# The last stage of a streaming encoder step: the last expert's rows added by 0/1 products, reloads moved behind expert 30, the sums on three engines

## The reference

```python
def _hmoe(x, g, w_router_group, w_router_expert, w_gate, w_up, w_down):
    xn = _rmsnorm(x, g).reshape(b * l, dm)
    ...                                   # each token picks 2 of the 8 experts of one of 4 groups
    y = jnp.zeros((n, dm), jnp.float32)
    for e in range(N_EXPERTS):            # 32 experts
        h = jax.nn.silu(xn @ w_gate[e]) * (xn @ w_up[e])
        y = y + combine[:, e:e + 1] * (h @ w_down[e]).astype(jnp.float32)
    return x + y.reshape(b, l, dm).astype(x.dtype)
...
return _rmsnorm(x, g_final), ...          # over all 544 rows
```

## Time and profile before

| | us |
|---|---|
| median of 3 runs | 889.67 (887.89 to 891.06) |
| the profiled execution, its span | 889.7 |
| TensorE busy | 799.5 (90%) |
| VectorE busy | 262.3 (29%) |
| GpSimd busy | 128.1 (14%) |
| ScalarE busy | 120.5 (14%) |
| last expert's result written by VectorE | 858.23 |
| the last stage's products on TensorE | 860.09 to 882.66 |
| last tile's row scaled | 886.57 |

### The profile page before, as it was taken

The page is one execution under the profiler, slowest core; times in us unless marked ns, Lnnn a source line. Parts: engine busy times, 40 slices in busy tenths (PEclk is TensorE's granted clock), DMA queues, the critical chain, the costliest instruction groups (busy, mean ns, idle before and its releaser), DMA issues.

```text
span 889.7 us, 9600 instructions
## 1 busy us (share of the span) xinstructions
PE 799.5 (90%) x3864; PEld 450.6 (51%) x3865; DVE 262.3 (29%) x734; ACT 120.5 (14%) x228; POOL 128.1 (14%) x224
## 2 busy tenths in 40 slices
PE   4999999999999999989999788779778877979876
PEld 4888888778888655533333233323323332323222
DVE  4799758310011355451111011111101101111115
ACT  5110021220000223400000000000000000000012
POOL 3000007840123300000111010010001001010000
PEclk9999999999999999989999898999889889999999
DMA  9622022253200393477999999999999999999965
GB/s 288 165 95 95 20 88 64 86 187 131 95 1 0 146 430 140 160 291 278 429 426 428 425 426 427 427 427 426 427 426 428 426 427 425 427 422 407 416 233 245
DMA packets 44688, 251.59 MB, mean 283 GB/s; under 512 B 13397, under 2 KB 14249, under 8 KB 32194
## 3 DMA queue, kind: packets, MB, share of 16 engines
q1 hardware_dynamic: 37682, 237.57, 65.8%
q0 software_dynamic: 6672, 12.86, 4.1%
q10 hardware_dynamic: 288, 0.53, 0.2%
HBM read 245.33 MB, written 13.46 MB: 291 GB/s over the span
## 4 chain that ended last, share of the span: by engine, by line
PE 60%; DMA 33%; SPq 4%; DVE 1%; issue 1%; ACT 0%; POOL 0%; DVEq 0%; ACTq 0%; POOLq 0%
DMA arena<-in_w_exp_up 28%; PE ps L1435 26%; PE ps L1702 12%; PE ps L1575 6%; PE ps L1717 5%; SPq L438 3%; PE ps L1789 3%; DMA arena<-x_rows 2%; DMA x_rows<-arena 1%; PE ps L1515 1%; PE ps L1510 1%; DMA arena<-in_x_prompt 1%; PE ps L1406 1%; PE ps L1692 1%; PE ps L1564 1%; SPq L442 1%
## 5 line engine op out<-in xcount | busy, mean ns | idle before, releaser
L1702 PE MATMUL ps<-arena 128*64 128x512 f32 x1024 | 249.7, 643 | 60.4 <-DMA arena<-in_w_exp_up 60.3
L1435 PE MATMUL ps<-arena 128*128 128x272 f32 x992 | 229.8, 393 | 0.0
L1435 PEld LDWEIGHTS ps<-arena 128*128 128x128 f32 x992 | 188.4, 190 | 38.1
L1702 PEld LDWEIGHTS ps<-arena 128*64 128x64 f32 x1024 | 82.7, 148 | 205.1 <-issue 197.0
L1717 PE MATMUL ps<-arena 128*64 128x512 f32 x512 | 116.5, 596 | 2.0 <-DVE arena L1333 2.0
L1337 DVE TENSOR_SCALAR arena<-ps,arena 128x512 f32<-128x512 f32 x32 | 24.0, 751 | 202.4 <-PE ps L1717 202.4
L814 DVE TENSOR_TENSOR arena<-arena 128x256 f32<-128x256 f32 (+11 forms) x217 | 74.6, 344 | 11.2 <-ACT arena L723 3.9
L1717 PEld LDWEIGHTS ps<-arena 128*64 128x64 f32 x512 | 37.6, 137 | 65.2 <-issue 60.8
L1302 DVE TENSOR_TENSOR arena<-ps,arena 128x1024 f32<-128x1024 f32 x15 | 18.4, 1225 | 176.4 <-PE ps L1692 176.4
L580 POOL DMA_INDIRECT y_parts<-arena x32 | 31.9, 998 | 241.2 <-DVE arena L1337 241.2
L764 ACT ACTIVATE arena<-ps,arena 128x512 f32<-128x512 f32 x32 | 22.0, 687 | 311.7 <-PE ps L1702 311.7
(11 more groups left out here) (229 smaller groups left out, 503.9 us busy)
## 6 DMA issues: line engine op xcount, KB each, us to landing
arena<-in_w_exp_gate SPq DMA_DIRECT2D x29, 2048.0 KB, 42.7
arena<-in_w_exp_up SPq DMA_DIRECT2D x29, 2048.0 KB, 32.5
arena<-in_w_exp_down SPq DMA_DIRECT2D x29, 2048.0 KB, 37.9
arena<-in_w_in SPq DMA_DIRECT2D x6, 2048.0 KB, 9.2
arena<-in_w_exp_gate SPq DMA_DIRECT2D x12, 512.0 KB, 12.8
arena<-in_w_exp_up SPq DMA_DIRECT2D x12, 512.0 KB, 19.2
arena<-in_w_exp_down SPq DMA_DIRECT2D x6, 1024.0 KB, 19.0
arena<-in_x_prompt SPq DMA_DIRECT2D x8, 512.0 KB, 6.4
```

The source lines that it names most:

```text
L1435: last = pe.matmul(dst[:, hh, 0:HALF], w[:, k, m * P:(m + 1) * P], rhs[:, k, hh * HALF:(hh + 1) * HALF], start=(k == 0), stop=(k == kk - 1))
L1702: last = pe.matmul(ps[n * TILE:(n + 1) * TILE, 2 + par, :], x_t[:, k, :], w[:, k, :], start=(k == 0), stop=(k == KD - 1))
```

## The change

1. y_parts is filled with zeros early, by nine DMAs on GpSimd's queue, once the first weight block is in.
2. Expert 31's rows are no longer scattered. VectorE keeps them in y_sb[1]. A 0/1 matrix `picks` (128 x 544) is made by VectorE: the entry at a slot and a token is 1 if the slot holds the token. GpSimd writes the token numbers for it by an iota, and two small VectorE instructions ahead of the expert loop give each slot's token. TensorE multiplies `picks` with y_sb[1], in two products for a tile, one on partitions 0 to 63 and one on 64 to 127 (`pick`), for all five tiles.
3. SyncE waits for the scatters of the experts up to 30 and then reloads y_parts.
4. The sums are shared: sample tile: GpSimd adds both expert halves to x2, TensorE picks, VectorE adds the two. Tiles 0 and 1: VectorE adds the two expert halves (`add_pair`), TensorE adds x2, the pick and the pair. Tile 2: GpSimd adds one half to x2, VectorE the other, TensorE adds pick and this sum. Tile 3: GpSimd adds one half to x2, TensorE adds pick, the other half and this sum.
5. The mean comes out of ScalarE's square (scale 1/32) and its root gets the epsilon as bias, so VectorE's mean instruction goes. The tiles end in the order 0, 4, 1, 2, 3 instead of 4, 0, 1, 2, 3.

```diff
-END_ORDER = (4, 0, 1, 2, 3)
+LOAD_ORDER = (4, 0, 1, 2, 3)
+END_ORDER = (0, 4, 1, 2, 3)
...
             sp.wait_ge(y_all, 1)
-            for par in range(2):
-                sp.wait_ge(y_stored[par], 16 * NP)
-            for i in END_ORDER:
+            sp.wait_ge(y_stored[0], 16 * NP)
+            sp.wait_ge(y_stored[1], 16 * (NP - 1))
+            for i in LOAD_ORDER:
...
+            pool.wait_ge(w_stream[0], 16)
+            by_part = y_parts.rearrange("(p n) c -> p (n c)", p=P)
+            span = 4 * NT * F // P
+            for c in range(0, span, D):
+                w = min(D, span - c)
+                pool.dma_start(by_part[:, c:c + w], zeros[:, 0:w]).then_inc(parts_zeroed, 16)
...
+            step(pool.memset(eps_col, EPS))
...
+                if e == NE - 1:
+                    break
+                if e == NE - 2:
+                    pool.wait_ge(gu_done, NE - 1)
+                    pool.iota(token_no, pattern=[[1, NT]], base=0, channel_multiplier=0,
+                              allow_small_or_imprecise_dtypes=True).then_inc(token_no_ready, 1)
                 pool.wait_ge(y_ready, e + 1)
...
+            pool.wait_ge(x2_back, 32)
+            pool.wait_ge(y_back[4], 16)
+            for k in range(2):
+                x_i = x2_end[4][:DEC]
+                pool.tensor_tensor(x_i, x_i, y_end[4][:DEC, k * D:(k + 1) * D], ALU.add).then_inc(sample_rows, 1)
+                pool.wait_ge(sample_rows, k + 1)
+            for i in (2, 3):
+                pool.wait_ge(y_back[i], 16)
+                pool.tensor_tensor(x2_end[i], x2_end[i], y_end[i][:, 0:D], ALU.add).then_inc(rows_added, 1)
...
                 act.activation(junk2[:r].rearrange("p (h n) -> p h n", h=2), src,
-                               ACT.Square, accum_out=ss[:r, i:i + 1]).then_inc(squares3, 1)
-                act.wait_ge(mean3, n + 1)
-                act.activation(rstd[:r, i:i + 1], ss[:r, i:i + 1], ACT.Sqrt).then_inc(root3, 1)
+                               ACT.Square, scale=1.0 / 32, accum_out=ss[:r, i:i + 1]).then_inc(squares3, 1)
+                act.wait_ge(squares3, n + 1)
+                act.activation(rstd[:r, i:i + 1], ss[:r, i:i + 1], ACT.Sqrt, bias=eps_col[:r]).then_inc(root3, 1)
...
+            ts(last_i, y_row[:, NE - 1:NE], 2, ALU.logical_shift_right)
+            step(dve.tensor_copy(last_token, last_i))
...
+                if e == NE - 1:
+                    dve.wait_ge(token_no_ready, 1)
+                    dve.tensor_scalar(picks, token_no, last_token, None, ALU.is_equal).then_inc(picks_ready, 1)
...
+            def add_pair(i):
+                dve.wait_ge(y_back[i], 16)
+                dve.tensor_tensor(y_end[i][:, 0:D], y_end[i][:, 0:D], y_end[i][:, D:2 * D], ALU.add).then_inc(pair_sum, 1)
...
+            add_pair(0)
+            add_pair(1)
+            dve.wait_ge(sample_rows, 2)
+            dve.wait_ge(sample_picked, 1)
+            sample = x2_end[4][:DEC].rearrange("p (h n) -> p h n", h=2)
+            dve.tensor_tensor(sample, ps[:DEC, 6:8, :], sample, ALU.add).then_inc(sample_sum, 1)
             dve.wait_ge(g_in, 32)
+            final(0)
+            dve.wait_ge(rows_added, 1)
+            dve.tensor_tensor(x2_end[2], x2_end[2], y_end[2][:, D:2 * D], ALU.add).then_inc(pair_sum, 1)
+            for n in range(1, TT):
+                final(n)
...
+            def pick(i, bank, first, end):
+
+                r = ROWS[i]
+                for half in range(2):
+                    rows = slice(half * TILE, (half + 1) * TILE)
+                    last = pe.matmul(ps[:r, bank + half, :], picks[rows, i * P:i * P + r], y_sb[1][rows, :], start=first, stop=end)
+                return last
+
+            pe.wait_ge(picks_ready, 1)
+            pick(4, 6, True, True).then_inc(sample_picked, 1)
+            pe.wait_ge(x2_back, 32)
+            for i in range(2):
                 add(i, x2_end[i], True, False)
-            for i in END_ORDER[1:]:
-                pe.wait_ge(y_back[i], 16)
-                add(i, y_end[i][:, 0:D], False, False)
-                add(i, y_end[i][:, D:2 * D], False, True).then_inc(sum_done, 1)
+                pick(i, 2 * i, False, False)
+            for i in range(2):
+                pe.wait_ge(pair_sum, i + 1)
+                add(i, y_end[i][:, 0:D], False, True).then_inc(sum_done, 1)
+            pick(2, 4, True, False)
+            pe.wait_ge(sample_sum, 1)
+            pick(3, 6, True, False)
+            pe.wait_ge(pair_sum, 3)
+            add(2, x2_end[2], False, True).then_inc(sum_done, 1)
+            pe.wait_ge(y_back[3], 16)
+            add(3, y_end[3][:, D:2 * D], False, False)
+            pe.wait_ge(rows_added, 2)
+            add(3, x2_end[3], False, True).then_inc(sum_done, 1)
```

More of the change, by code:

```diff
@@ L219, in encoder_step @@
         junk2 = ring[1][:, 0:D]
+        token_no, picks = ring[3][:, 0:NT], ring[3][:, NT:2 * NT]
         places = [[O_MISC + M_PAR, O_MISC + M_SS], [O_CPOW + SLOT, O_D], [O_UT + SLOT, O_GC],
@@ L260, in encoder_step @@
         ov_tab, ov_unused = small(4), small(1)
+        last_i, last_token, eps_col = small(1).bitcast(I32), small(1), small(1)
         ov_y_row, ov_x_row = small(1).bitcast(I32), small(1).bitcast(I32)
@@ L521, in _ @@
             pool.wait_ge(rows_zeroed, 16)
+            pool.wait_ge(parts_zeroed, 16 * (-(-4 * NT * F // P // D)))
             pool.wait_ge(h_ready_y, 2)
@@ L584, in put_entries @@
             def put_entries():
-                for par in range(2):
-                    pool.wait_ge(y_stored[par], 16 * NP)
+                pool.wait_ge(y_stored[0], 16 * NP)
+                pool.wait_ge(y_stored[1], 16 * (NP - 1))
+                pool.wait_ge(y_ready, NE)
                 pool.sem_inc(ov_done, 1)
@@ L1359, in _ @@
             overflow(dve, more)
-            dve.wait_ge(g_in, 32)
-            dve.wait_ge(x2_back, 32)
-            last = END_ORDER[0]
-            dve.wait_ge(y_back[last], 16)
-            for k in range(2):
-                x_i = x2_end[last][:ROWS[last]]
-                dve.tensor_tensor(x_i, x_i, y_end[last][:ROWS[last], k * D:(k + 1) * D], ALU.add).then_inc(sample_sum, 1)
-                dve.wait_ge(sample_sum, k + 1)
-            for n, i in enumerate(END_ORDER):
-                r = ROWS[i]
-                dve.wait_ge(squares3, n + 1)
-                mean, root_i = ss[:r, i:i + 1], rstd[:r, i:i + 1]
-                dve.tensor_scalar(mean, mean, 1.0 / D, EPS, ALU.mult, ALU.add).then_inc(mean3, 1)
-                dve.wait_ge(mean3, n + 1)
-                dve.wait_ge(root3, n + 1)
-                inverse_root(mean, root_i)
-                x_i, g_i = (x.rearrange("p (h n) -> p h n", h=2) for x in (x2_end[i][:r], g_end[:r]))
-                dve.scalar_tensor_tensor(out=x_i, in0=ps[:r, 2 * i:2 * i + 2, :] if n else x_i, scalar=root_i,
-                                         in1=g_i, op0=ALU.mult, op1=ALU.mult).then_inc(final_ready, 1)
+            dve.wait_ge(x2_back, 32)
@@ new lines, in add_pair, with final @@
+            def add_pair(i):
+                dve.wait_ge(y_back[i], 16)
+                dve.tensor_tensor(y_end[i][:, 0:D], y_end[i][:, 0:D], y_end[i][:, D:2 * D], ALU.add).then_inc(pair_sum, 1)
+            def final(n):
+                i = END_ORDER[n]
+                r = ROWS[i]
+                dve.wait_ge(root3, n + 1)
+                mean, root_i, tmp = ss[:r, i:i + 1], rstd[:r, i:i + 1], misc(M_SS + 16, 1, r)
+                step(dve.reciprocal(root_i, root_i))
+                tt(tmp, root_i, root_i, ALU.mult)
+                stt(tmp, mean, EPS, tmp, ALU.add, ALU.mult)
+                ts(tmp, tmp, -0.5, ALU.mult, 1.5, ALU.add)
+                tt(root_i, root_i, tmp, ALU.mult)
+                x_i, g_i = (x.rearrange("p (h n) -> p h n", h=2) for x in (x2_end[i][:r], g_end[:r]))
+                dve.scalar_tensor_tensor(out=x_i, in0=x_i if i == 4 else ps[:r, 2 * i:2 * i + 2, :], scalar=root_i,
+                                         in1=g_i, op0=ALU.mult, op1=ALU.mult).then_inc(final_ready, 1)
@@ L1784, in _ @@
             overflow(pe, more)
-            pe.wait_ge(x2_back, 32)
+            pe.wait_ge(y_all, 1)
             def add(i, part, first, end):
```

22 lines of the change are left out of this document (12 added, 10 removed).

## The result

| | before | after |
|---|---|---|
| median, us | 889.89 (887.89 to 891.06, 4 runs) | 894.84 (893.76 to 895.66, 4 runs) |
| ratio, 95% interval | | 1.0047 (1.0031 to 1.0063) |
| span of the profiled execution | 889.7 | 892.1 |

The changed kernel is 0.47% slower by this ratio (the two medians differ by 0.56%); the forecast was 888.0, 0.19% faster, with a range up to 890.8. 894.84 lies outside it.

A forecast was written before the change was run, and what follows sets the result against it. The last stage was taken as bound by TensorE. Waiting until 875.0 for the third pair_sum, its last pass starts at 879.7 and the span ends at 887.1; 0.9 for VectorE being held gives 888.0 us, range 885.0 to 890.8.

The forecast's parts named there:

- picks in pairs: TensorE's last stage: the two half-row products of a pick run side by side, 0.86 us plus a 0.15 change.
- reloads issued: SyncE's y_parts reloads, no longer waiting for expert 31, are issued at about 854 instead of 862.9.
- last reload lands: The y_parts reload of tile 3 lands at 873.0; before, the last tile landed at 876.4.
- mixer rows land: The mixer rows' load ahead of the last stage lands at 860.04, the same as before.
- tile 0 scaled, from there: Scaling of tile 0 on ScalarE and VectorE: 3.9 us less 0.22, from 870.0 to 873.7.
- third pair_sum, held for: VectorE's add for tile 2, wanted at 873.7, may be held by GpSimd's tile 3 add: 0.9 of 1.4 us.
- 12 passes, first to last start: TensorE's last three adds after its wait run from 875.0 to a last pass starting at 879.7.
- VectorE and GpSimd: Last stage: either engine may hold the other on two-input SBUF operations; counted at one place, 0.9 of 1.4 us.
- Rival C: TensorE's wait of 1.6 to 3.0 us is followed by half clock, costing up to 1.7 us: 889.7; chance 0.11.
- A: Last stage: reloads land early and the clock does not fall, so the end comes at 885.3; chance 0.27.
- B: TensorE's pick halves do not run side by side, five times 0.86 us more, giving 890.5; chance 0.06.
- D: Kernel start: the zero fill delays the small loads at 19.57, giving 896.9 at worst; chance 0.06.

The follow-up runs named there:

- e5: The changed kernel with the reloads issued only when the mixer rows are in; 894.97 us, ratio 1.0048 to the kernel before.
- e3: The changed kernel with the scaling's small products rewritten to one tensor input and a scalar; 890.30 us, ratio 0.9996 to the kernel before.
- e4: The changed kernel with GpSimd's four adds given to VectorE and TensorE, small two-input products kept; 891.96 us, ratio 1.0013 to the kernel before.
- e9: The kernel before plus 12 unneeded two-input GpSimd adds of 128x1024 over the last stage; 897.68 us, a single execution.
- e10: The kernel before plus 12 unneeded one-input GpSimd operations in the last stage; 905.5 us, a single execution.
- e6: The changed kernel with TensorE adding tile 3's expert half before waiting for the third pair_sum; 891.32 us, ratio 1.0006 to the kernel before.
- e1: The kernel before with only the early zero fill of y_parts added; 889.81 us, ratio 0.9989 to the kernel before.
- e7: The changed kernel with one-input scaling forms, all picks but tile 3's before the mixer rows, third pair_sum given to TensorE; 889.61 us, ratio 0.9988 to the kernel before.

## Why the prediction was wrong

Its steps, from R (before: the earlier trace rows, R = 858.23):

| step | forecast | after | difference |
|---|---|---|---|
| picks in pairs | 0.86 + 0.15 | 1.06 | none |
| reloads issued | R-4.2 | R-5.7 | -1.5 (worth nothing, e5) |
| last reload lands | R+14.8 | R+15.9 | +1.1 |
| mixer rows land | R+1.8 | R+3.9 | +2.1 |
| tile 0's sum ready for ScalarE | R+11.8 | R+13.6 | +1.8 |
| tile 0 scaled, from there | 3.7 | 6.0 | +2.3 |
| third pair_sum, held for | 0.9 | 0 | -0.9 |
| 12 passes, first to last start | 4.7 | 6.5 | +1.8 |
| last pass to end | 7.4 | 7.5 | +0.1 |

The last five rows are one path (the ones above them feed it), and their sum is 5.1 us, against 34.8 - 29.8 = 5.0. (The last reload is at 873.0 and 873.2 in the times of the traces; R came 0.9 us earlier. TensorE did not wait for it, but GpSimd's add of tile 3 follows it at 873.25, and that is the add which holds the product of 2.00.) Of the 6.8 us between 888.0 and 894.84 the rest is the 1.6 that lies outside the span, and -0.9 and +1.1 by which R came earlier in the profiled execution and the median lies above it.

**The step that failed** is "VectorE and GpSimd", where the text says of the hold: "It counts at one place: VectorE's third pair_sum, wanted at 873.7". The mechanism was right and its price for the pair_sum in the right range (e3: 0.45). The place was wrong. GpSimd's adds of 870.4 to 875.1 were worked out in the same prediction, and the scaling of tile 0 (870.0 to 873.7) lies inside them; but I had priced that scaling as one piece, "From ACT's start to VectorE's end are 3.9 us", read from a stage in which GpSimd did nothing. Inside the piece are three products with two SBUF inputs of 0.16 us, and in the changed kernel two of them take 0.54 and 2.00, 2.2 us more. I looked for long VectorE operations, when a held one costs what is left of the other's. e3 and e4 remove this in two different ways, and e9 makes it alone.

The Trainium skill, "SBUF — State Buffer", section "SBUF: two separate sides", states the rule that decided: whichever of the two starts first has the port pair for its whole instruction and the other is fully blocked. e9's rows agree, and so do the scalings with an input in PSUM (1.28, not held). By that rule, applied to every two-input VectorE instruction and not to one, the hold was worth the 2.2 us more. e10's row does not agree for a one-input GpSimd operation: the one hold seen ends about 1.05 us into its 2.77, and there the measurement decides.

**Rival C** was priced rightly ("up to 1.7", measured 7.1 - 5.4 = 1.7) and given too little chance, 0.11: its condition was a wait "as long as that gap", and the wait that I had at 1.6 to 3.0 us became 3.6. The prediction's own sign of C, a half clock past 873, is the one that came. The two errors have one cause: the lock lengthens the wait, and the longer wait was followed by half clock. e3 removes both at once, e6 only the second. That the wait's length decides late in the stage rests on three waits with and three without.

**The mixer rows** landed 2.1 us later, since the reloads shared the engines with them; I had left their landing unchanged by not asking what an early transfer does to the one before it. This feeds the +1.8 of tile 0's sum. What it cost at the end is not shown by itself: e5 takes it away, but there another hold, of VectorE's first add, stands in its place. The last reload did land 2.3 us earlier behind R than in the kernel before, and e5 has the same landing with the reloads issued at R+1.9 (R+4.7 before). So no longer waiting for expert 31's scatter is enough for those 2.3 us, and issuing them another 7.6 us earlier added nothing. In the changed kernel the DMA share falls to 0.30 from 864 on, in e5 it is 1.02 from 866 to 870, and the last landing is the same. So the amount that all engines together have to move did not set it; a few late engines would, but no view here shows a single engine.

**Rivals A, B, D.** A had the clock staying up and the reloads early; the clock fell at the start in both profiled executions of the changed kernel, the last reload came at R+15.9, and the mixer rows came late. B is out by the 1.06 us of a pick. D is out by e1.

**What stays open.** Why half clock follows the gap of 2.4 to 2.7 us at the start of the stage in some executions and not in others. And e3 ends at R+32.0, 0.5 behind the kernel before when its clock fell too (R+31.5) and 1.0 when it did not; the rest of the wait (2.0) and the late mixer rows are the candidates. e7 takes away that wait and fills the time of the late mixer rows with picks, and is 2.2 us better than e3 with the same fall of the clock, but the two were not taken apart. No run has the changed kernel's late wait with the full clock forced, so the 1.7 us of half clock are read from e3 and not isolated.

## What to carry to other kernels

Before giving GpSimd adds in a stage where VectorE is busy, list every VectorE instruction with two SBUF inputs that can fall beside them, the 0.16 us ones above all: each can cost a whole GpSimd instruction (2.35 us here). Where the second operand is one value a partition, pass it as the scalar of a one-input form. And before a transfer is issued earlier, ask what its landing really waits for and what it delays: here 7.6 us or more of earlier issue did not move the last landing and cost the load ahead 2.0 us.

## What the runs showed of the hardware

- A VectorE product of 128x1 takes 0.16 us alone and up to 2.35 beside a GpSimd add of 128x1024; as a form with a scalar from SBUF it takes 0.21 and is not held.
- VectorE's scaling over 1024 columns takes 1.28 us with one input in PSUM, beside a GpSimd add or not; with both inputs in SBUF it took 3.00 beside one (e9) and 1.27 alone.
- GpSimd's add of 128x1024 f32 takes 2.35 us from two different inputs and 1.89 with the same input twice (e9); a one-input product of the same size is slower, 2.77 (e10).
- ScalarE's root with a bias takes 0.30 us against 0.20 without.
- Reloads issued about 8 us earlier behind R landed at the same place (last one R+15.9 and R+15.7) and made the load of the mixer rows ahead of them 23.4 us long instead of 21.4.
